# Input projection: the norm's factor at the copy-out, x turned by column quarters under the first weight tile

## The reference, cut to what matters

```python
def rms_norm(x, g):
    y = x * lax.rsqrt(jnp.mean(x * x, axis=-1, keepdims=True) + EPS)
    return y * g
z = rms_norm(x, norm_g) @ w_in          # x: 560 rows of 2048; w_in: 2048 x 6152
```

## Time and profile before

| | |
|---|---|
| median of 3 runs | 4167.3 us (4165.81 to 4169.4) |
| the profiled execution, its own time | 4173.99 us |
| its span, first to last instruction | 4172.0 us |
| TensorE busy, share of the span | 91% |
| VectorE busy, ScalarE busy | 48%, 30% |
| mean granted TensorE clock | 0.949 |

### The profile page before, as it was taken

How to read it: one execution, slowest core, us unless ns; L and a number is a source line. 1 busy time by engine, 2 the same in 40 slices (tenths; PEclk the granted TensorE clock), 3 DMA queues, 4 the chain that set the end, 5 groups by cost and what they waited for, 6 DMA issues and landing times. The chain is left out here.

```text
span 4172.0 us, 69083 instructions
## 1 busy us (share of the span) xinstructions
PE 3789.4 (91%) x26984; PEld 3472.0 (83%) x26984; DVE 2014.3 (48%) x2660; ACT 1258.5 (30%) x1530; POOL 19.6 (0%) x50
## 2 busy tenths in 40 slices
PE   5999996675878899999997899999999999999998
PEld 4999995454677777667774799999999999999998
DVE  5222222694546778788886524333333333333333
ACT  2111111243103666666665223121121121121121
POOL 0000000000000000000000000000000000000000
PEclk8999998887968999999998999999999999999999
DMA  5444341415446678788877332222222222222221
GB/s 145 110 106 111 105 113 45 148 39 160 109 148 226 226 269 294 272 282 288 290 269 250 104 85 71 91 81 83 88 80 84 87 80 88 83 80 90 81 80 63
DMA packets 459388, 574.17 MB, mean 138 GB/s; under 512 B 38150, under 2 KB 333108, under 8 KB 458156
## 3 DMA queue, kind: packets, MB, share of 16 engines
q1 hardware_dynamic: 459260, 572.54, 43.6%
HBM read 521.68 MB, written 50.80 MB: 137 GB/s over the span
## 5 line engine op out<-in xcount | busy, mean ns | idle before, releaser
L67 PE MATMUL f_acc<-hidden_hi,ffn_lo 128*128 128x280 f32 x2048 | 603.1, 294 | 11.2 <-DVE hidden_lo L2331 11.2
L67 PE MATMUL f_acc<-xf_hi,ffn_lo 128*128 128x280 f32 x2048 | 598.2, 292 | 0.6
L69 PE MATMUL f_acc<-hidden_hi,ffn_hi 128*128 128x280 f32 x2048 | 598.7, 292 | 0.0
L68 PE MATMUL f_acc<-hidden_lo,ffn_hi 128*128 128x280 f32 x2048 | 597.7, 292 | 0.0
L69 PE MATMUL f_acc<-xf_hi,ffn_hi 128*128 128x280 f32 x2048 | 595.6, 291 | 0.0
L68 PE MATMUL f_acc<-xf_lo,ffn_hi 128*128 128x280 f32 x2048 | 594.6, 290 | 0.0
L67 PE MATMUL z_acc<-xn_hi,win_lo 128*128 128x280 f32 x1536 | 450.9, 294 | 19.3 <-DVE xn_lo L232 19.3
L69 PE MATMUL z_acc<-xn_hi,win_hi 128*128 128x280 f32 x1536 | 450.7, 293 | 0.0
L68 PE MATMUL z_acc<-xn_lo,win_hi 128*128 128x280 f32 x1536 | 449.4, 293 | 0.0
L2300 ACT ACTIVATE ffn_hi<-ffn_raw 128x2048 fp32r<-128x2048 f32 x127 | 242.3, 1908 | 637.2 <-PE f_acc L69 637.2
L67 PEld LDWEIGHTS f_acc<-hidden_hi,ffn_lo 128*128 128x128 f32 x2048 | 386.1, 189 | 16.0 <-DVE hidden_lo L2331 14.9
(11 more groups left out here) (328 smaller groups left out, 6298.9 us busy)
## 6 DMA issues: line engine op xcount, KB each, us to landing
dc_pages<-in_cache_k SPq DMA_DIRECT2D x256, 512.0 KB, 4.7
dc_pages<-in_cache_v SPq DMA_DIRECT2D x256, 512.0 KB, 5.2
ffn_raw<-in_w_up SPq DMA_DIRECT2D x64, 1024.0 KB, 6.3
ffn_raw<-in_w_down SPq DMA_DIRECT2D x64, 1024.0 KB, 5.0
win_raw<-in_w_in SPq DMA_DIRECT2D x48, 1024.0 KB, 6.3
ffn_raw<-in_w_out SPq DMA_DIRECT2D x16, 1024.0 KB, 6.6
z_scratch<-z_out SPq DMA_DIRECT2D x48, 280.0 KB, 2.4
sm_c<-in_state_C SPq DMA_DIRECT2D x32, 256.0 KB, 5.0
```

What stands on the lines that cost most here:

```text
L67: nc.tensor.matmul(out, wlo, xhi, start=first, stop=False)
L68: nc.tensor.matmul(out, whi, xlo, start=False, stop=False)
L69: return nc.tensor.matmul(out, whi, xhi, start=False, stop=last)
```

## The change

- **The factor 1/rms** no longer goes on x. It is put on z when a tile is copied out of PSUM: the copy becomes a multiplication by `rstd` (`dve_copy_out`). Each block of x needs only the gain: VectorE makes `hi` as xt x gain (`x_leading`) and `lo` as xt x gain - hi (`x_trailing`). ScalarE's split of x goes away.
- **The sum of squares** is taken from x as it was loaded, rows on partitions: ScalarE squares half a row (1024 columns of 112 rows) with a running sum, ten times (`squares`, in `ORDER`), four of them between evacuations and six behind the split of weight tile 1. VectorE adds the halves, ScalarE takes the root, VectorE the reciprocal, all on 5 columns. Five diagonal matrices and five matmuls with ones spread the 560 factors over the partitions, and two copies bring them to `rstd`.
- **x is loaded in column quarters**: 28 transfers with rows of 2 KB, and a semaphore for each quarter. The gain and weight tile 0 are issued ahead of them, weight tile 1 behind them. Two of the five row buffers have memory of their own (`x_rows`), so that `raw[0]` and `raw[1]` are free from the start; tiles 2 and 3 wait until x is turned and six of the ten squares are made.
- **TensorE** turns quarter 0; then it turns block k and at once makes all 6 matmuls of tile 0 (both halves) for block k - 4. Tile 1 is made in two halves, with the spread of the factors between them. **ScalarE** alone evacuates the turned blocks. `NormBuffers` and its five functions go away.

```diff
-class NormBuffers:
...
-def embed_and_project(nc, d, a, sems, ident, xhi, xlo, xt_dram, z_dram):
+def embed_and_project(nc, d, a, sems, ident, ones, xhi, xlo, xt_dram, z_dram):
...
+    QUARTER = d.kc // 4
...
-        xrow = lambda t: flow.raw[0:d.tt, t, :] if t < GROUP else \
+        xfree = sb("x_rows", [P, 2, d.dm])
+        xrow = lambda t: xfree[0:d.tt, t, :] if t < 2 else flow.raw[0:d.tt, t, :] if t < GROUP else \
             zc[0:d.tt, :, :].rearrange("p j t -> p (j t)")[:, 0:d.dm]
         xt = sb("xt", [P, d.kc, d.t])
         gain = sb("norm_mix_cols", [P, d.kc])
-        norm = NormBuffers(nc, ctx, d, sems, "mix", sb("mix_sq", [P, 2, d.t]), acc[1])
+        square = sb("x_square", [P, d.dm // 2])
+        ssq = sb("x_ssq", [P, 2, d.nt])
+        inv, root = sb("x_inv", [P, d.nt]), sb("x_root", [P, d.nt])
+        diag = sb("x_inv_diag", [P, d.nt, d.tt])
+        rstd = sb("x_rstd", [P, d.t])
         turned = [ctx.enter_context(nc.psum_tensor(f"x_turned{i}", [P, 2, 512], F32)) for i in range(2)]
-        rows_in, gain_in = sems("x_rows_in"), sems("norm_mix_in")
-        turned_ready, xt_ready, xt_tail, xt_stored = (sems(n) for n in (
-            "x_turned_ready", "xt_ready", "xt_tail", "xt_stored"))
+        rows_in, gain_in = [sems(f"x_rows_in{q}") for q in range(4)], sems("norm_mix_in")
+        turned_ready, xt_ready, xt_stored, x_hi, x_lo = (sems(n) for n in (
+            "x_turned_ready", "xt_ready", "xt_stored", "x_hi", "x_lo"))
+        ssq_made, meaned, rooted, inverted, diag_made, spread_made, rstd_made = (sems(f"x_{n}") for n in (
+            "ssq_made", "meaned", "rooted", "inverted", "diag_made", "spread_made", "rstd_made"))
+        ORDER = [(0, 2), (0, 3), (0, 0), (0, 1), (1, 2), (1, 3), (0, 4), (1, 0), (1, 1), (1, 4)]
         split = 4 * d.tt
         n_last = d.seq - split + N_META
         assert d.nt == GROUP + 1
...
         @block.sync
         def _(sp):
             x = a["x_prompt"][0]
+            samples = a["x_sample"].rearrange("b s m -> (b s) m")
             head = d.tt - N_META
-            sp.dma_start(xrow(0)[0:N_META, :], a["meta_tokens"]).then_inc(rows_in, 16)
-            sp.dma_start(xrow(0)[N_META:d.tt, :], x[0:head, :]).then_inc(rows_in, 16)
-            for t in range(1, d.nt - 1):
-                r0 = head + (t - 1) * d.tt
-                sp.dma_start(xrow(t), x[r0:r0 + d.tt, :]).then_inc(rows_in, 16)
-            sp.dma_start(xrow(d.nt - 1)[0:n_last, :], x[d.seq - n_last:d.seq, :]).then_inc(rows_in, 16)
-            sp.dma_start(xrow(d.nt - 1)[n_last:d.tt, :], a["x_sample"].rearrange("b s m -> (b s) m")).then_inc(rows_in, 16)
             sp.dma_start(gain[:, :], a["norm_mix"][0].rearrange("(k p) -> p k", p=P),
                          allow_slow_non_contiguous=True).then_inc(gain_in, 16)
+            sp.dma_start(raw[0], w[:, :, 0:P]).then_inc(flow.landed[0], 16)
+            for q in range(4):
+                cs = slice(q * QUARTER * P, (q + 1) * QUARTER * P)
+                sp.dma_start(xrow(0)[0:N_META, cs], a["meta_tokens"][:, cs]).then_inc(rows_in[q], 16)
+                sp.dma_start(xrow(0)[N_META:d.tt, cs], x[0:head, cs]).then_inc(rows_in[q], 16)
+                for t in range(1, d.nt - 1):
+                    r0 = head + (t - 1) * d.tt
+                    sp.dma_start(xrow(t)[:, cs], x[r0:r0 + d.tt, cs]).then_inc(rows_in[q], 16)
+                sp.dma_start(xrow(d.nt - 1)[0:n_last, cs], x[d.seq - n_last:d.seq, cs]).then_inc(rows_in[q], 16)
+                sp.dma_start(xrow(d.nt - 1)[n_last:d.tt, cs], samples[:, cs]).then_inc(rows_in[q], 16)
+            sp.dma_start(raw[1], w[:, :, P:2 * P]).then_inc(flow.landed[1], 16)
             sp.wait_ge(turned_ready, d.kc)
-            for j in range(GROUP):
+            sp.wait_ge(ssq_made, ORDER.index((1, GROUP - 1)) + 1)
+            for j in range(2, GROUP):
                 sp.dma_start(raw[j], w[:, :, j * P:(j + 1) * P]).then_inc(flow.landed[j], 16)
-            sp.wait_ge(xt_ready, d.kc)
-            sp.wait_ge(xt_tail, d.kc)
+            sp.wait_ge(xt_ready, 2 * d.kc)
             sp.dma_start(xt_dram.rearrange("(k p) t -> p k t", p=P), xt[:, :, :]).then_inc(xt_stored, 16)
             sp.dma_start(gate_raw[:, :, :], w[:, :, n_tiles * P:d.pw]).then_inc(gate_in, 16)
             with sp.Fori(0, n_tiles // GROUP - 1) as g:
@@ -320,15 +256,32 @@
 
         @block.scalar
         def _(act):
-            for k in range(d.kc):
+            def evacuate(k):
                 act.wait_ge(turned_ready, k + 1)
-                nc.scalar.activation(xt[:, k, split:d.t], turned[k % 2][:, 1, 0:d.t - split], ACT.Copy).then_inc(xt_tail, 1)
-
-            def first_tiles():
-                for j in range(2):
-                    act.wait_ge(flow.landed[j], 16)
-                    leading(j)
-            norm_scalar(nc, act, d, norm, xhi, first_tiles)
+                nc.scalar.activation(xt[:, k, 0:split], turned[k % 2][:, 0, 0:split], ACT.Copy).then_inc(xt_ready, 1)
+                nc.scalar.activation(xt[:, k, split:d.t], turned[k % 2][:, 1, 0:d.t - split],
+                                     ACT.Copy).then_inc(xt_ready, 1)
+
+            def squares(first, last):
+                for n in range(first, last):
+                    h, t = ORDER[n]
+                    if n:
+                        act.wait_ge(ssq_made, n)
+                    nc.scalar.activation(square[0:d.tt, :], xrow(t)[:, h * d.dm // 2:(h + 1) * d.dm // 2], ACT.Square,
+                                         accum_out=ssq[0:d.tt, h, t:t + 1]).then_inc(ssq_made, 1)
+
+            act.wait_ge(flow.landed[0], 16)
+            leading(0)
+            for q in range(4):
+                for k in range(QUARTER * q, QUARTER * (q + 1)):
+                    evacuate(k)
+                if q in (1, 2):
+                    squares(2 * q - 2, 2 * q)
+            act.wait_ge(flow.landed[1], 16)
+            leading(1)
+            squares(4, len(ORDER))
+            act.wait_ge(meaned, 2)
+            nc.scalar.activation(root[0:d.tt, :], inv[0:d.tt, :], ACT.Sqrt).then_inc(rooted, 1)
             act_group(act, 0, True)
             with act.Fori(1, n_tiles // GROUP) as g:
                 act_group(act, g * GROUP, False)
@@ -338,8 +291,9 @@
         def dve_copy_out(dve, n, j, rows=P):
             dve.wait_ge(flow.used, n + 1)
             for h in range(2):
-                nc.vector.tensor_copy(zc[0:rows, j, h * d.half:(h + 1) * d.half],
-                                      acc[j % 2][h][0:rows, 0:d.half]).then_inc(copied, 1)
+                cols = slice(h * d.half, (h + 1) * d.half)
+                nc.vector.tensor_tensor(zc[0:rows, j, cols], acc[j % 2][h][0:rows, 0:d.half],
+                                        rstd[0:rows, cols], ALU.mult).then_inc(copied, 1)
 
         def trailing(dve, n, j):
             dve.wait_ge(flow.hi_made, n + 1)
@@ -356,21 +310,40 @@
                 if nth + (j > 0) >= 1:
                     dve_copy_out(dve, i + j - 1, (j - 1) % GROUP)
 
-        def square(dve, k):
-            dve.wait_ge(xt_ready, k + 1)
-            dve.wait_ge(xt_tail, k + 1)
-            norm_square(nc, dve, norm, xt, k)
+        def x_leading(dve, k):
+            dve.wait_ge(xt_ready, 2 * k + 2)
+            nc.vector.tensor_scalar(xhi[:, k, :], xt[:, k, :], gain[:, k:k + 1], None, ALU.mult).then_inc(x_hi, 1)
+
+        def x_trailing(dve, k):
+            dve.wait_ge(x_hi, k + 1)
+            nc.vector.scalar_tensor_tensor(xlo[:, k, :], xt[:, k, :], gain[:, k:k + 1],
+                                           xhi[:, k, :].bitcast(F32), ALU.mult, ALU.subtract).then_inc(x_lo, 1)
 
         @block.vector
         def _(dve):
+            trailing(dve, 0, 0)
+            dve.wait_ge(gain_in, 16)
             for k in range(d.kc):
-                dve.wait_ge(turned_ready, k + 1)
-                nc.vector.tensor_copy(xt[:, k, 0:split], turned[k % 2][:, 0, 0:split]).then_inc(xt_ready, 1)
-                if k >= 1:
-                    square(dve, k - 1)
-            square(dve, d.kc - 1)
-            dve.wait_ge(gain_in, 16)
-            norm_scale(nc, dve, d, norm, xt, gain, xhi, xlo, lambda: [trailing(dve, j, j) for j in range(2)])
+                x_leading(dve, k)
+                if k % QUARTER:
+                    x_trailing(dve, k - 1)
+                if k % QUARTER == QUARTER - 1:
+                    x_trailing(dve, k)
+            trailing(dve, 1, 1)
+            dve.wait_ge(ssq_made, 2 * d.nt)
+            nc.vector.tensor_tensor(inv[0:d.tt, :], ssq[0:d.tt, 0, :], ssq[0:d.tt, 1, :], ALU.add).then_inc(meaned, 1)
+            dve.wait_ge(meaned, 1)
+            nc.vector.tensor_scalar(inv[0:d.tt, :], inv[0:d.tt, :], 1.0 / d.dm, EPS, ALU.mult, ALU.add).then_inc(meaned, 1)
+            dve.wait_ge(rooted, 1)
+            nc.vector.reciprocal(inv[0:d.tt, :], root[0:d.tt, :]).then_inc(inverted, 1)
+            dve.wait_ge(inverted, 1)
+            for t in range(d.nt):
```

(125 more changed lines are left out.)

8 lines of the change are left out of this document (removed).

## The result

The changed kernel takes 4181.41 us (median of 6 runs, 4174.15 to 4188.72); the kernel before, on the same chip, 4167.98 us (median of 6 runs, 4165.81 to 4169.4). The ratio is 1.0034 with a 95% interval of 1.0021 to 1.0047: slower by some 13 us, where 4118.5 us and 49 us faster were forecast. The profiled execution after took 4181.86 us, its span 4180.1 us, at a mean granted clock of 0.951.

What follows compares the result with a forecast made beforehand. Up to 112.2 us a chain of waits bounds the start, then TensorE the projection; tile 1 ending at 63.4 instead of 112.2 saves 48.8 us, so the 4167.3 median becomes 4118.5, range 4111 to 4130.

Steps and rivals of the forecast that it cites:

- The first transpose: Start of the projection: TensorE's first transpose at 17.5 us (16 to 19) instead of 27.23.
- Quarter 0 and the clock: Projection start: first four blocks turned at 21.2 us; TensorE at half clock until 27.5, full after.
- the rival of half clock through all of tile 0: Projection, tile 0: TensorE stays at half clock, saving only 37 to 43 us, about 4127; chance 0.17.
- The steps: Projection: twelve steps of turning block k with tile 0's block k - 4, 1.40 us each at full clock.
- The stops: Within the twelve steps: ScalarE twice stops evacuating for two squares, nothing to 2.66 us each, 2.7 charged in all.
- tile 0: Projection: the last four block steps, 3.1 us, end tile 0 at 46.6 us.
- Tile 1: Projection: factors at 56.5 us, TensorE waits 2.4, five small matmuls 0.7, tile 1 ends at 63.4.
- Behind it: Projection after tile 1: copy-outs cost nothing more, tile 4's weights have 14 us of slack, 12.3 us per tile.
- The step that failed: Before 112.2 us in the projection: whatever the change moves there shifts the rest of the program; saving 48.8 us.
- The last rival: Loading of x: 28 small transfers don't overlap, tile 1 ends at 37.8 + 28c; chance 0.03.
- c = 3.14: Loading of x: us per piece if each waits for the one before; tile 1 at 125.7, time 4180.8.

Runs made afterwards that it cites:

- the ninth experiment: Against the changed kernel with 12 tiny matmuls at the projection's start: all ten squares moved behind the last evacuation; 4121.27 us (one run).

## Why the prediction was wrong

**The first transpose** stood at 18.59 us for 17.5 (16 to 19). Transfers flowed at some 250 GB/s (252 from 12 to 18.6, 241 from there to 31), not at the 292 that I took; SP's first issue of x took 2.13 us.

**Quarter 0 and the clock.** Turned at 22.7 (its last transposes start at 22.31) for 21.2. The transposes of a row tile went from 0.39 to 0.26 us between 24.15 and 26.51, where 27.5 was forecast. That is 8 us after the first transpose, among transposes and matmuls mixed, so the rival of half clock through all of tile 0 fell; the rule of the Trainium skill (TensorE: Matmul & The Clock Gate, Part 4: PE-mode transpose), by which a transpose does not count as work for the clock "the same way", cost nothing that shows here; which of the two kinds the clock answered to, no run separates.

**The steps** took 1.25 to 1.28 us (35.51 to 36.76) for 1.40. **The stops** were the term most over-sized: 2.7 us charged, and a step with a stop took 1.71 (36.76 to 38.47) instead of 1.27, 0.9 us for both, as the ninth experiment confirms. VectorE idled for 0.87 and 0.76 us at the stops, and TensorE never waited for it there. Tile 1 started at 45.50, so **tile 0** ended at 44.4 for 46.6.

**Tile 1.** A square took 1.06 + 0.19 us with some overlap, 1.19 from one to the next, for 1.33; the factors' diagonals were ready at 52.7 for 56.5; TensorE waited 0.86 us for 2.4. The five small matmuls took 1.37 for 0.7. Tile 1 came out at 60.36 for 63.4: saving 51.85 for 48.8. **Behind it** the tiles follow one another at 12.32 us as forecast, with no gap at tile 2 or 4.

**The step that failed** is one sentence of the first part, on which the sum rests: that whatever the change moves before 112.2 "shifts the rest of the program". It did, to 49.57 us at the MLP's first matmul. But the change also takes 120 TensorE instructions out of the code, and with them the MLP's loop, 2400 us later, moved from place 96 to place 232 of a block. That cost 56.8 us: 41.1 us idle in two waits at each of 14 returns, and most of the rest, 13.1 us, in a longer busy time of the matmuls on `xf` beside and behind them (4.5, 3.6 and 5.0 us in L67, L68 and L69). 49.6 less 56.8 is the 7.2 us by which the last write of `hidden` comes later. The profiled executions differ by 7.9 us and the medians by 13.4, because the profiled execution of before stands 6.0 above that kernel's median of 4167.98. None of the rivals had this, since all of them looked for the loss inside the stage. The last rival, with 4180.8 us for c = 3.14, comes within 1 us of the measured time by luck: it wanted tile 1 at 125.7, which came out at 60.36. With the loop out of the bad place the same change takes 4121.36 or 4122.11 us, 3 to 4 above the forecast and inside its range; against the kernel before in the same sessions that is 53 us less, where 48.8 were forecast.

That the place of the loop is the cause is shown: by instruction count alone, in both kernels, in both directions, from two places in the code, and with the second wait moving as the place does. In every slow run a border also stands only 20 or 24 instructions behind the loop's start, and that alone could have been the cause. The trace of the changed kernel speaks against it. By the same count, each loop's body taken once, another TensorE loop (L1683, 275 instructions, written out six times in the code) has one of its copies at place 235, 21 ahead of a border, and touches 2 blocks. None of that line's branches lasts longer than 0.24 us, while the 14 taken branches of the MLP's loop (L2270) last 3.5 to 4.1, for 0.21 in the kernel before (ns, least, median and most, the loop's last branch, which is not taken, included):

```profile
L1683 PEldq COMPARE_BRANCH  x24: 76/211/236, 1273.7 to 2104.8; - x24
...
L2270 PEldq COMPARE_BRANCH  x15: 76/3801/4104, 2698.6 to 4155.0; - x15
```

The count can be off by a few instructions, and no run changed the length of the body, so that 7 blocks are the limit for other loops too is not shown. Nor is it shown why eight blocks are too many, when the 2048 instructions that the Trainium skill gives would be just eight; that the store also takes a block fetched ahead is only a guess, to which the 9 packets a return would fit.

## What to carry to other kernels

A change that adds or removes instructions moves every loop behind it on that engine; if a loop's body is about as long as this one's 7 blocks, count where it starts, and after the change look at the instruction queue's packets and at waits put down to "issue" before judging the change itself. Compare the time at which each later stage starts, in both traces: a gain that is still there 2400 us on and gone at the end names the stage that lost it. Here a dozen tiny matmuls where TensorE was idle anyway mended the loop at no cost that the time shows.
